# Squaring the second input tile on another engine, and adding an output group's earlier panels ahead, in a two-block transformer kernel

## The reference

```python
# first block
u = rmsnorm(h, norm_mix_g);  p = u @ w_in + b_in               # 7424 columns
merged = sigmoid(gate_a) * (attention(...) @ w_branch_attn) + sigmoid(gate_b) * (hgrn2(...) @ w_branch_hgrn)
h = h + merged @ w_out                                         # output group "out"
u = rmsnorm(h, norm_ffn_g)
h = h + (silu(u @ w_gate) * (u @ w_up)) @ w_ffn_down           # output group "down"
x = rmsnorm(h, norm_final_g)
# second block; mod = silu(c) @ w_ada + b_ada gives shifts, scales and gates
h = rmsnorm_2(x, norm_mix_w) * (1 + sc_m) + sh_m
x = x + g_m * (concat([y_ssd, y_att]) @ w_out_2)               # output group "oo"
h = rmsnorm_2(x, norm_ffn_w) * (1 + sc_f) + sh_f
x = x + g_f * (conv_ffn(h, ...) @ w_down_2)                    # output group "dd"
return rmsnorm_2(x, final_norm_w)
```

## Time and profile before

| | us |
|---|---|
| median of 3 runs | 803.60 (802.14 to 804.76) |
| the profiled execution | 801.52 |
| its span, first to last instruction | 799.8 |
| PE busy in it | 789.7 |
| DVE busy | 600.0 |
| ACT busy | 489.4 |

### The profile page before, as it was taken

How to read it: one execution, slowest core, us unless ns; L and a number is a source line. 1 busy time by engine, 2 the same in 40 slices (tenths; PEclk the granted TensorE clock), 3 DMA queues, 4 the chain that set the end, 5 groups by cost and what they waited for, 6 DMA issues and landing times. The chain is left out here.

```text
span 799.8 us, 14311 instructions
## 1 busy us (share of the span) xinstructions
PE 789.7 (99%) x5952; PEld 741.6 (93%) x5952; DVE 600.0 (75%) x809; ACT 489.4 (61%) x744; POOL 17.8 (2%) x38
## 2 busy tenths in 40 slices
PE   8999999999999999999999999999999999999996
PEld 8999979999999889999998889999789999999885
DVE  5576686677876868797878897987968787777463
ACT  6778888467743564443434357857758767666451
POOL 3000001000200000000000000001000000000000
PEclk9999999999999999999999999999999999999998
DMA  8873634556444558988887993734362756544711
GB/s 301 294 252 118 208 122 146 160 190 231 159 158 162 181 184 264 296 285 265 288 298 267 352 370 113 256 106 159 106 211 79 258 165 203 167 165 178 237 52 53
DMA packets 105680, 161.15 MB, mean 201 GB/s; under 512 B 4480, under 2 KB 51856, under 8 KB 105616
## 3 DMA queue, kind: packets, MB, share of 16 engines
q1 hardware_dynamic: 105472, 159.97, 59.8%
q10 hardware_dynamic: 144, 0.26, 0.1%
HBM read 159.16 MB, written 1.06 MB: 200 GB/s over the span
## 5 line engine op out<-in xcount | busy, mean ns | idle before, releaser
L1752 PE MATMUL ps<-p1H,wH 128*128 128x256 f32 x1256 | 358.4, 286 | 0.4 <-DVE p1L L1102 0.2
L1102 DVE TENSOR_TENSOR wL<-raw,wH 128x2048 fp32r<-128x2048 f32 (+2 forms) x142 | 284.4, 2008 | 97.7 <-ACT wH L705 94.2
L1752 PE MATMUL ps<-p1H,wL 128*128 128x256 f32 x1256 | 354.8, 283 | 0.0
L1752 PE MATMUL ps<-p1L,wH 128*128 128x256 f32 x1256 | 353.4, 283 | 0.0
L705 ACT ACTIVATE wH<-raw 128x2048 fp32r<-128x2048 f32 (+1 forms) x114 | 212.0, 1864 | 135.9 <-PE ps L1752 79.8
L1752 PEld LDWEIGHTS ps<-p1H,wH 128*128 128x128 f32 x1256 | 240.8, 192 | 3.6 <-issue 2.0
L1752 PEld LDWEIGHTS ps<-p1H,wL 128*128 128x128 f32 x1256 | 240.8, 192 | 0.0
L1752 PEld LDWEIGHTS ps<-p1L,wH 128*128 128x128 f32 x1256 | 240.1, 192 | 0.1
L1755 PE MATMUL ps<-wH,zH 128*128 128x512 f32 x168 | 65.4, 389 | 0.0
L1755 PE MATMUL ps<-wH,zL 128*128 128x512 f32 x168 | 65.4, 389 | 0.0
L1755 PE MATMUL ps<-wL,zH 128*128 128x512 f32 x168 | 65.4, 389 | 0.0
(11 more groups left out here) (295 smaller groups left out, 997.1 us busy)
## 6 DMA issues: line engine op xcount, KB each, us to landing
raw<-in_w_in SPq DMA_DIRECT2D x37, 1024.0 KB, 5.2
raw<-in_w_ada SPq DMA_DIRECT2D x24, 1024.0 KB, 5.3
raw<-in_w_up SPq DMA_DIRECT2D x44, 512.0 KB, 4.8
raw<-in_w_ffn_gate SPq DMA_DIRECT2D x22, 512.0 KB, 4.4
raw<-in_w_ffn_up SPq DMA_DIRECT2D x22, 512.0 KB, 5.7
raw<-in_w_ffn_down SPq DMA_DIRECT2D x10, 1024.0 KB, 5.2
raw<-in_w_down SPq DMA_DIRECT2D x10, 1024.0 KB, 5.2
raw<-in_w_out SPq DMA_DIRECT2D x8, 1024.0 KB, 5.0
```

The source lines that it names most:

```text
L1102: return v.tensor_tensor(o, a, b, op)
L1752: last = mm(ps[:, t[1], 0:T], wt[:, slot, k, t[2]:t[2] + P], at_[:, k0 + k, :], start=st, stop=en)
```

## The change

Start: x's tile 0 comes in two DMAs of 512 columns each, tile 1 in one; SP issues the weights after the first of the three has landed. VectorE squares tile 1, in one SCALAR_TENSOR_TENSOR with a sum over 1024 columns, ahead of its first reciprocal; ScalarE squares tile 0 alone, and copies the first transposed block (`first_turned`) between its first and second root. PE's two warming products between the tiles' transposes go.

Output groups: a new function `all_but_last_part` on VectorE adds tile 1's own bank, which now holds all panels but the last, to the residual. It is called in `evac` of the i = 1 group ahead of tile 0's addition. The left column half of the last panel goes to bank 7 with this panel alone, the right one to bank 6 as before, and `last_tile` adds each once. `HALVES` gets an event for either bank. In group dd `turn_over(4, 0)` moves from before the right half's addition to behind it, as it already was in oo.

Besides: `squares` counts one less (tile 1's first square has a semaphore of its own), and a semaphore of the SSD norm is merged into another (`yrt` into `yln`), which changes no order.

```diff
-        on.in_x = [ctx.enter_context(nc.semaphore(f"in_x{j}")) for j in range(TB)]
+        on.in_x = [ctx.enter_context(nc.semaphore(f"in_x{b}")) for b in range(3)]
...
-        HALVES = {"out1": EV["bh1", 2], "down1": (on.tmp_done, 16), "oo1": (on.pt_done, 9), "dd1": EV["u9", 2]}
+        HALVES = {"out1": (EV["bh1", 3], EV["bh1", 2]), "down1": ((on.ada_done, 4), (on.tmp_done, 16)),
+                  "oo1": ((on.pt_done, 9), (on.pt_done, 9)), "dd1": (EV["u9", 3], EV["u9", 2])}
...
         def _(sp):
-            for j in range(TB):
-                sp.dma_start(res[:, j], IN["x"][0, j * P:(j + 1) * P, :]).then_inc(on.in_x[j], 16)
+            for i in range(2):
+                sp.dma_start(res[:, 0, half(i)], IN["x"][0, 0:P, half(i)]).then_inc(on.in_x[i], 16)
+            sp.dma_start(res[:, 1], IN["x"][0, P:2 * P, :]).then_inc(on.in_x[2], 16)
             sp.wait_ge(on.in_x[0], 16)
...
-            def square_x(j):
-
-                act.wait_ge(on.in_x[j], 16)
-                if j:
-                    act.wait_ge(on.sq_done, j)
-                nc.scalar.activation(xsq, res[:, j], ACT.Square, accum_out=XS[:, 1, j:j + 1]).then_inc(on.sq_done, 1)
+            def square_x():
+
+                act.wait_ge(on.in_x[0], 16)
+                act.wait_ge(on.in_x[1], 16)
+                nc.scalar.activation(xsq, res[:, 0], ACT.Square, accum_out=XS[:, 1, 0:1]).then_inc(on.sq_done, 1)
...
+                elif n == 0 and j:
+                    act.wait_ge(on.sq_x1, 1)
...
+            def first_turned(n):
+
+                act.wait_ge(on.ut_psum, 4 * n + 1)
+                nc.scalar.activation(TMP[:, 0], un(0), ACT.Copy).then_inc(on.un0_copy, 1)
...
+                    elif j == 0:
+                        square_x()
                     else:
-                        square_x(j)
+                        first_turned(n)
                     root(n, j)
                 if n == 4:
                     return
-                act.wait_ge(on.ut_psum, 4 * n + 1)
-                nc.scalar.activation(TMP[:, 0], un(0), ACT.Copy).then_inc(on.un0_copy, 1)
+                if n:
+                    first_turned(n)
...
             def norm(n):
                 if n == 0:
+                    dve.wait_ge(on.in_x[2], 16)
+                    v.scalar_tensor_tensor(out=xsq1, in0=res[:, 1], scalar=1.0, in1=res[:, 1], op0=ALU.mult, op1=ALU.mult,
+                                           accum_out=XS[:, 1, 1:2]).then_inc(on.sq_x1, 1)
                     turn_over(n, 0)
...
+            def all_but_last_part(name, n):
+
+                whole, o = res[:, 1, half(1)], ps[:, GROUPS[name]["tiles"][1][1], :]
+                dve.wait_ge(*USED[PIDX[name, len(GROUPS[name]["parts"]) - 2]])
+                if n < 3:
+                    step(tt(whole, o, whole, ALU.add))
+                else:
+                    dve.wait_ge(*EV[name[:2] + "0", 1])
+                    step(tt(gt, o, GATE[n - 3][1], ALU.mult))
+                    step(tt(whole, gt, whole, ALU.add))
+
             def last_tile(name, n):
 
                 left, right = res[:, 1, W:W + T], res[:, 1, W + T:D]
-                o, o2 = ps[:, GROUPS[name]["tiles"][1][1], :], ps[:, 6, 0:T]
+                o1, o2 = ps[:, 7, 0:T], ps[:, 6, 0:T]
                 dve.wait_ge(on.half_done, HALF[n])
                 if n < 3:
-                    tt(left, o[:, 0:T], left, ALU.add).then_inc(on.res_half, 1)
-                    step(tt(right, o[:, T:W], right, ALU.add))
+                    tt(left, o1, left, ALU.add).then_inc(on.res_half, 1)
...
                     dve.wait_ge(*EV[name, 0])
-                    if n == 3:
-                        step(tt(gt, o, g, ALU.mult))
-                        tt(res[:, 1, half(1)], gt, res[:, 1, half(1)], ALU.add).then_inc(on.res_half, 1)
-                    else:
-                        step(tt(gt[:, 0:T], o[:, 0:T], g[:, 0:T], ALU.mult))
-                        tt(left, gt[:, 0:T], left, ALU.add).then_inc(on.res_half, 1)
-                        step(tt(gt[:, T:W], o[:, T:W], g[:, T:W], ALU.mult))
-                        step(tt(right, gt[:, T:W], right, ALU.add))
-                        turn_over(n, 0)
+                    step(tt(gt[:, 0:T], o1, g[:, 0:T], ALU.mult))
+                    tt(left, gt[:, 0:T], left, ALU.add).then_inc(on.res_half, 1)
                     dve.wait_ge(on.res_half, PART[n])
                     dve.wait_ge(on.tile_done, TILE[name, 1])
                     step(tt(gt[:, 0:T], o2, g[:, T:W], ALU.mult))
                     tt(right, gt[:, 0:T], right, ALU.add).then_inc(on.evac_dve, 1)
-                    if n == 3:
-                        turn_over(n, 0)
+                    turn_over(n, 0)
...
                     for j in range(TB):
                         hb, o = res[:, j, half(i)], ps[:, GROUPS[name]["tiles"][j][1], :]
+                        if n in HALF and i and not j:
+                            all_but_last_part(name, n)
                         if n in HALF and i and j:
                             last_tile(name, n)
                             continue
...
                 if n == 0:
-                    pe.wait_ge(on.in_x[j], 16)
+                    for b in ((0, 1), (2,))[j]:
+                        pe.wait_ge(on.in_x[b], 16)
...
                     if half_of is not None:
-                        bank, st = (t[1], False) if half_of == 0 else (6, k == 0)
+                        bank, st = 7 - half_of, k == 0
...
+                        if final and m == 1 and name in HALVES:
+                            pe.wait_ge(*HALVES[name][0])
                         for k in range(nk):
...
-                            pe.wait_ge(*HALVES[name])
+                            pe.wait_ge(*HALVES[name][1])
...
                     for j in range(TB if n == 0 else 0):
-                        warm(4 - 2 * j)
+                        if j == 0:
+                            warm(4)
                         stream_in(0, 0, j)
```

More of the change, by code:

```diff
@@ L112, in squares @@
 def squares(n, x):
-    return 4 * n - 2 + x
+    return 4 * n - 3 + x
 def slot(nh, hh):
@@ L313, in build @@
         on.hat_zero = ctx.enter_context(nc.semaphore("hat_zero"))
+        on.sq_x1 = ctx.enter_context(nc.semaphore("sq_x1"))
         on.sq_done = ctx.enter_context(nc.semaphore("sq_done"))
@@ L361, in build @@
         on.yTh = ctx.enter_context(nc.semaphore("yTh"))
-        on.yrt = ctx.enter_context(nc.semaphore("yrt"))
         on.ysq = ctx.enter_context(nc.semaphore("ysq"))
@@ L447, in build @@
         UR, UC = scr(30, 4, T + 2), scr(36, 4, T)
-        sqj, gt, xsq = scr(60, W), scr(62, W), scr(60, D)
+        sqj, gt, xsq, xsq1 = scr(60, W), scr(62, W), scr(60, D), scr(56, D)
         gfin, gout = scr(64, D), scr(40, D)
@@ L774, in root @@
                     act.wait_ge(on.ysq_done, 4)
+                elif n == 0 and j:
+                    act.wait_ge(on.sq_x1, 1)
                 else:
-                    act.wait_ge(on.sq_done, squares(n, 3 + j) if n else 1 + j)
+                    act.wait_ge(on.sq_done, squares(n, 3 + j) if n else 1)
                 if n in HALF and j:
@@ L1081, in _ @@
                     act.wait_ge(on.yln, 1)
-                    nc.scalar.activation(sT[:, 0], sT[:, 0], ACT.Exp, scale=-0.5).then_inc(on.yrt, 1)
+                    nc.scalar.activation(sT[:, 0], sT[:, 0], ACT.Exp, scale=-0.5).then_inc(on.yln, 1)
                 elif k == "store":
@@ L1646, in _ @@
                     dve.wait_ge(on.yz, 4)
-                    dve.wait_ge(on.yrt, 1)
+                    dve.wait_ge(on.yln, 2)
                     def low(t):
@@ L1734, in panel @@
                 final = part == len(g["parts"]) - 1
+                split_last = name in HALVES and part == len(g["parts"]) - 2
                 if q > 1 and not (part == 1 and name in NORM_OF):
@@ L1749, in product @@
                         st = part == 0 and k == 0 and x == 0
-                        en = final and k == nk - 1 and x == 2
+                        en = k == nk - 1 and x == 2 and (final or split_last and t is g["tiles"][1])
                         if t[0] == "cm":
```

## The result

| | before | after |
|---|---|---|
| median, same chip, 8 runs each | 802.58 (801.88 to 804.76) | 806.21 (804.15 to 807.91) |
| ratio | | 1.0041, 95% interval 1.0029 to 1.0052 |
| the profiled execution | 801.52 | 807.48 |
| its span | 799.8 | 805.8 |
| mean granted clock of PE | 0.997 | 0.995 |

The change makes the kernel 0.4% slower, about 3.3 to 3.6 us. The range of the forecast, 802.4 to 807.2 around 805.0, holds the median, but the sum behind it was +1.4, and more than twice as much was lost. The rest needs an account of its own.

The account below looks back on a forecast made before the run. TensorE, with work during 99% of the span, was taken to bound the kernel. Terms 0.05 + 0.56 + 0.15 + 0.90 - 0.25 = +1.4 us on a median of 803.60 gave 805.0, eight-in-ten range 802.4 to 807.2.

Parts of the forecast that it names:

- Joint 1: Row norm after out1: the new add delays tile 0's add and the second spread; PE loses 0.56 us.
- Joint 3: Row norm after oo1: the new multiply and add delay the left and final pairs on DVE; +0.90 us, all on PE.
- One of the signs: Forecast wrong if PE's wait at oo1's norm is under 0.6; about 1.1 was expected, 0.24 before.
- Tail: After dd1's last product: the final pair starts earlier, but ACT's scaling delays its last square; -0.25 us, ends 0 and -0.3.
- Joint 2: Row norm after down1: new add from 478.54 makes the second reciprocal 0.42 later; PE loses 0.15 us.
- Start: Kernel start: second root +0.15 later, about 0.10 returned by earlier weights; +0.05 us, from -0.6 to +0.35.
- I leave the landing at 5.65: Start: x's tile 1 lands at 5.65 despite its later issue, since the same megabyte stands in the queue.
- Rival C: Start: a PE pause puts off its clock's rise past the first products; up to +0.8, total +2.2, 805.8; chance 0.10.
- ACT's copy end at 7.05: Start: PE turns tile 1 by about 6.7, ACT's copy ends about 7.05, and the root stands at 7.0 to 7.15.
- my 1.35: Start: DVE's accumulating square of tile 1 takes 1.35 us, between ends of 1.04 and 1.50.
- Rival B: Start: DVE's accumulating square takes 1.1 longer, each element at twice the cost; total +2.5, 806.1; chance 0.10.
- The sum: Whole kernel: start, three joints and tail add up to +1.4 us, giving 805.0 from the median 803.60.

Follow-up runs that it names:

- Experiment 3: The changed kernel with the new add called ahead of the weight split and of before(n) in out1 and oo1; median 804.6, ratio 1.0022 to before.
- 6: The kernel before with the change's start alone, but the two warming products between the tiles kept; median 803.1, ratio 1.0012 to before.
- 12: The changed kernel with tile 0's reciprocal in the tail taken before the right half's last multiply and add again; median 805.3, ratio 1.0038 to before.
- 10: The kernel before with the change's start, but x in two DMAs and the two warming products kept; median 802.2, ratio 0.9996 to before.
- 2: Groups alone: the changed kernel with the start as it was before; median 803.4, ratio 1.0018 to before.
- experiment 8: Groups alone, with adds hoisted in out1 and oo1, down1's evacuation ahead of the next weight split, tail reciprocal before the last pair; median 802.4, ratio 1.0000 to before.
- 4: The changed kernel with the split of the next group's weights moved from ahead of down1's evacuation into norm 2; median 804.9, ratio 1.0024 to before.
- 1: Start alone: the kernel before with the change's start, output groups as before; median 803.5, ratio 1.0008 to before.
- experiment 5: Start alone, but SP asks for the weights only when both DMAs of x's tile 0 have landed; median 803.6, ratio 1.0010 to before.
- 9: The kernel before with the change's start, warming products gone, but x in two DMAs as before; median 802.5, ratio 1.0005 to before.

## Why the prediction was right or wrong

**Joint 1: right.** +0.56 forecast, +0.47 measured; reciprocal, right add and spread are within 0.1 of the forecast places once the 0.17 of the start is added. Experiment 3 undoes it.

**Joint 3: right.** +0.90 forecast, +0.83 measured (0.84 once) in the five kernels that have the pair there, +0.09 in the two where it is hoisted. One of the signs that I had set for being wrong is met all the same: PE's wait before the second pair is 0.56, under 0.6 (and at joint 1 it is 0.22, not some 0.5). I had read the whole loss as one wait. It comes in two, since the first pair of spreads now waits too (0.25, at 608.71), for tile 0's reciprocal, which moved by the same 0.84 against PE; and a row counts the wait from the modelled end of the matmul before, while the pair behind each wait is 0.10 longer. By starts it is plain: from the last transposing matmul to the second pair it is 0.73 in before and 1.57 in after. So the sign was badly set, and the term held.

**Tail: right.** -0.25 forecast with an end at -0.3; -0.30 to -0.35 measured. The square moved by 0.17, the upper of the two places given, and the part behind the last add gave 0.17, which I had put under 0.1. The reason was right too: taking the reciprocal back ahead of the last pair gives the other 0.4.

**Joint 2: the mechanism right, the size wrong.** The step put the new add at 478.54, right behind DVE's split, as if the split's end were fixed. It hangs on the landing of weight panels. The kernel before had two covers here, 0.30 of DVE's idle time before tile 0's add and 0.34 between the second reciprocal and PE's need for it. The new add takes 0.72. With the split in time that leaves 0.08 for PE, under the 0.15 forecast; but each tenth by which the split comes late now falls on PE. The panel landed at 476.24 in before and at 478.48 in after, and the split came 1.89 late, when the 0.31 that PE was late by then is taken off: 1.89 + 0.72 - 0.30 = 2.31 for the second reciprocal (2.30 measured), and 0.34 less is PE's loss, 1.97 (1.98 measured). The same sum fits the other traces. In groups alone the split came 0.20 late and 0.30 was lost. The start with later weights has no new add: 1.30 late, 0.67 lost. Start alone: 0.55 late, nothing lost, under the old cover. In 6 and 12 it was the panel ahead that landed late and held both splits, by 0.90 and 1.09: the sum gives 0.26 (without the new add) and 1.17, and both were measured. The rows of 12, DVE and then ACT:

```profile
478.47 3.43 DVE L1112 TENSOR_TENSOR wL<-raw,wH 128x2048 fp32r<-128x2048 f32 x2 [1.01 <-ACT wH L707]
...
476.52 1.92 ACT L707 ACTIVATE wH<-raw 128x2048 fp32r<-128x2048 f32 x1 [1.38 <-DMA raw<-in_w_in]
```

So joint 2 cost 0.3 to 2 and not 0.15. The term that was mis-sized is this scatter of a transfer that had just been early enough; the sum put it at nothing. It may also be why the two halves of the change cost more together than apart, which no run here settles: the start's kernels are the ones with the late panels (last section), and the groups' edit eats the cover over them.

**The clock behind joint 2: not foreseen, and not tied to either half of the change.** Of fourteen traces seven have a stretch at half clock there, five of 6.8 us (3.1 to 3.2 lost) and two of 3.4 (1.6). Experiments 6 and 10 have no edit of the groups, experiments 2 and 8 none of the start, and experiment 8 no loss at the joint, and all four have it; 4 lost 1.44 and had the short one, 12 lost 1.17 and had none. Before's 98 executions beside the experiments fall in two heaps, 60 with a mean clock above 0.995 (medians 801.6 to 802.0) and 38 at or below (803.8 to 804.8). I read those of the second heap as having this stretch, since in the fourteen traces the seven with it have a mean clock of 0.993 to 0.995 and the seven without one of 0.997 to 0.999. Neither trace of before has the stretch, so that is argued, not shown, and in kernel 12 the heaps lie only 0.6 apart (805.7 for six executions, 805.1 for five), which this reading doesn't explain. By it, comparing one profiled execution of each kernel (+5.97) says too much: 38 of 98 executions of before would lose as much or half of it too. What is left, 2.77, is short of the +3.3 to +3.6 of the medians; the start, cheap in this one execution, is likely the rest.

**Start: wrong in three places, by luck unseen in the first trace.** The forecast was +0.05, with an upper end of +0.35; the four other traces with this start whole (1, 3, 4 and 12) lost 1.30 to 2.07. (1) "I leave the landing at 5.65": with x in three DMAs tile 1 landed at 6.22 to 6.73 in six traces of seven, the seventh being after's; with two, at 5.50 to 5.69 in seven of seven. In experiment 5, asking for the weights 0.6 later didn't help; why a DMA issued 0.5 later lands 0.6 to 1.1 later than in before stays open. (2) Rival C, the clock, which I gave 0.10, was the case. Without the two products the first rise came at 11.6 to 12.9 in six traces of seven, at 5.7 in after's; with them at 5.9 to 8.7 in seven of seven. After's rise came as early as the missing products would have run (from 5.30 in before), so there they had hardly a part in it. Experiments 9 and 10 differ in these products alone, 12.0 against 8.7, in one trace each. Its price, +0.8, was about right: +1.0 in experiment 9. The Trainium skill, TensorE: Matmul & The Clock Gate, section "What's actually happening", has the throttled clock as the default, released by activity, and says the same kernel changes over at different points in different runs; the traces agree on both (matmuls 0.21 apart at first in all of them, and with the same start a rise at 5.7 in after and at 12.7 in 12). (3) I let ACT's copy end at 7.05 with the root right behind it. That held where the transposes were early; where they were late the root waited for PE, 0.7 behind the sum in 10 and 0.2 in 1 and 9, against 0.04 in after.

DVE's square itself was cheap: 1.226 and a read of 0.083, against my 1.35. Rival B fell with it, and with it the rule of the Trainium skill, Vector Engine (DVE) Microarchitecture Reference, "Points that are easy to get wrong", that two such sources halve the throughput: 1024 columns with a sum took 1.226, a plain 128x1024 of the same engine 1.23 (479.60 in joint 2's rows).

**The sum.** With the start at the +1.3 to +2.1 of the five other traces that have it (experiment 5 with later weights among them), joint 1 +0.47, joint 2 +0.3 to +2, joint 3 +0.83 and the tail -0.34, after should cost 2.6 to 5.1 where the start goes so, and 1.5 to 2.2 less where it goes as in after's trace. The median of 12 at +3.3 and of after at +3.6 lie within. The forecast of +1.4 was short by start and joint 2. Its 805.0 lay nearer to 806.2 than its reasoning deserved, since it started from a median (803.60 of three runs) that was 1.0 above that of more runs (802.58).

## What to carry to other kernels

Work moved ahead of time is free only if it is ahead of what the engine's queue is waited for: the same add cost 0.47 or nothing, by its place. Where an edit eats the last cover of a joint, price the scatter of each transfer that ends just before it, from several traces if there are some, and never from the one in which it came in time. At a start, products that only keep TensorE busy and the number of DMAs are part of the schedule; taking one away has to be priced as a clock that comes late, and a waiting copy placed ahead of a root as a new wait.

## What the runs showed of the hardware

- The first rise of PE's clock moved by 3 us or more on two small products more or less between the transposes of x (5.9 to 8.7 with, 11.6 to 12.9 without, one exception).
- Behind joint 2, where PE does 32-column sums and four spreads, the clock fell to half in seven of fourteen traces, and no pause of PE was needed for it (kernel 8). With two 512-column products ahead none of 12 executions had a low mean clock, but three kernels without them had only one of 12.
- The weight panel that decides joint 2 took 6.8 to 7.1 us from issue to landing in the kernels with x in two DMAs and 7.3 to 8.7 in those with three. It is one of the 212 transfers besides x that all fourteen traces have. Five of them separate so cleanly, three in the first 18 us, this one, and one near 716 that goes the other way; chance alone would give about a tenth of one (an estimate, 212 x 2 / 3432, if they were independent). I take it as a hint and leave the cause open.
